# End of the down projection: joins of the first columns as transfers, the last product by tiles of 128 rows, final scaling on three engines

## The reference

```python
def rms_norm(x, gain):
    xf = x.astype(jnp.float32)
    y = xf * lax.rsqrt(jnp.mean(xf * xf, axis=-1, keepdims=True) + NORM_EPS)
    return (y * gain.astype(jnp.float32)).astype(x.dtype)

def squared_relu_mlp(h, w_up, w_down):          # w_down: 8192 x 2048
    u = jax.nn.relu(jnp.einsum('bsd,df->bsf', h, w_up))
    return jnp.einsum('bsf,fd->bsd', u * u, w_down)

    x = x + squared_relu_mlp(h, w_mlp_up[layer], w_mlp_down[layer])
return rms_norm(x, ln_final)
```

## Time and profile before

| | before |
|---|---|
| median of 3 runs | 2839.78 us (2839.66 to 2840.45) |
| the profiled execution's own time | 2841.27 us |
| its span | 2839.8 us |
| granted TensorE clock, mean | 0.997 |
| TensorE busy | 2801.2 us (99%) |
| VectorE busy | 1884.5 us (66%) |
| ScalarE busy | 1181.7 us (42%) |
| GpSimd busy | 345.2 us (12%) |
| last matmul starts | 2823.47 us |
| last of the eight final scalings ends | 2834.99 us |

### The profile page before, as it was taken

The page is one execution under the profiler, slowest core; times in us unless marked ns, Lnnn a source line. Parts: engine busy times, 40 slices in busy tenths (PEclk is TensorE's granted clock), DMA queues, the critical chain, the costliest instruction groups (busy, mean ns, idle before and its releaser), DMA issues.

```text
span 2839.8 us, 42734 instructions
## 1 busy us (share of the span) xinstructions
PE 2801.2 (99%) x16624; PEld 2424.8 (85%) x16624; DVE 1884.5 (66%) x2073; ACT 1181.7 (42%) x1375; POOL 345.2 (12%) x400
## 2 busy tenths in 40 slices
PE   8999999999999999999999999999999999999997
PEld 5888777788889988889888899999998788888886
DVE  7545777755454443434445788888863888888888
ACT  5433433433454332423334365555553333333334
POOL 4000000000001123200111421212113100000001
PEclk9999999999999999999999999999999999999999
DMA  5333222232347874423333699999987756656555
GB/s 164 96 86 93 75 68 79 64 82 78 111 137 212 234 217 122 169 90 110 129 118 110 211 249 258 246 250 246 252 240 256 257 195 221 222 207 221 207 215 132
DMA packets 466144, 477.78 MB, mean 168 GB/s; under 512 B 10832, under 2 KB 369264, under 8 KB 465904
## 3 DMA queue, kind: packets, MB, share of 16 engines
q1 hardware_dynamic: 427136, 346.66, 39.9%
q0 software_dynamic: 38896, 129.56, 15.6%
HBM read 366.60 MB, written 81.79 MB: 158 GB/s over the span
## 4 chain that ended last, share of the span: by engine, by line
PE 91%; DVE 4%; DMA 2%; ACT 2%; issue 1%; POOL 0%; SPq 0%; DVEq 0%; ACTq 0%
PE slab_ps L1004 12%; PE slab_ps L1006 12%; PE slab_ps L1005 12%; PE down_ps L1651 7%; PE down_ps L1653 6%; PE down_ps L1652 6%; PE mix_ps L1594 6%; PE mix_ps L1593 6%; PE mix_ps L1595 6%; PE mix_ps L1006 2%; PE mix_ps L1005 2%; PE mix_ps L1004 2%; PE down_ps L1004 2%; PE down_ps L1006 2%; PE down_ps L1005 2%
## 5 line engine op out<-in xcount | busy, mean ns | idle before, releaser
L1004 PE MATMUL slab_ps<-act_hi,w_hi 128*128 128x512 f32 (+2 forms) x1928 | 721.4, 374 | 15.4 <-DVE act_lo L2421 10.6
L1006 PE MATMUL slab_ps<-act_hi,w_lo 128*128 128x512 f32 (+2 forms) x1928 | 698.5, 362 | 0.0
L1005 PE MATMUL slab_ps<-act_lo,w_hi 128*128 128x512 f32 (+2 forms) x1928 | 698.4, 362 | 0.0
L1679 ACT ACTIVATE w_hi<-w_raw 128x2048 fp32r<-128x2048 f32 x152 | 290.9, 1914 | 550.3 <-PE slab_ps L1006 414.9
L2369 DVE TENSOR_TENSOR w_lo<-w_raw,w_hi 128x2048 fp32r<-128x2048 f32 x152 | 349.4, 2298 | 233.4 <-ACT w_hi L1679 232.7
L1004 PEld LDWEIGHTS slab_ps<-act_hi,w_hi 128*128 128x128 f32 (+1 forms) x1928 | 364.0, 189 | 80.3 <-issue 23.7
L1006 PEld LDWEIGHTS slab_ps<-act_hi,w_lo 128*128 128x128 f32 (+1 forms) x1928 | 363.9, 189 | 57.9 <-issue 1.0
L1005 PEld LDWEIGHTS slab_ps<-act_lo,w_hi 128*128 128x128 f32 (+1 forms) x1928 | 364.4, 189 | 54.7 <-issue 5.3
L1651 PE MATMUL down_ps<-half_hi,u_slot 128*128 128x512 f32 x896 | 350.1, 391 | 2.6 <-DMA u_slot<-u_park 2.6
L1653 PE MATMUL down_ps<-half_lo,u_slot 128*128 128x512 f32 x896 | 349.9, 391 | 0.0
L1652 PE MATMUL down_ps<-half_hi,u_slot 128*128 128x512 f32 x896 | 349.8, 390 | 0.0
(11 more groups left out here) (484 smaller groups left out, 4889.7 us busy)
## 6 DMA issues: line engine op xcount, KB each, us to landing
b<-in_w_mlp_down_dram SPq DMA_DIRECT2D x64, 1024.0 KB, 6.7
w_raw<-in_w_in_dram SPq DMA_DIRECT2D x56, 1024.0 KB, 5.6
u_slot<-u_park SPq DMA_DIRECT2D x112, 512.0 KB, 8.4
w_raw<-in_w_mlp_up_dram SPq DMA_DIRECT2D x84, 512.0 KB, 7.8
w_raw<-in_w_cross_kv_dram SPq DMA_DIRECT2D x32, 1024.0 KB, 6.4
u_park<-u_hi POOLq DMA_DIRECT2D x32, 896.0 KB, 6.4
u_park<-u_lo POOLq DMA_DIRECT2D x32, 896.0 KB, 10.1
ucomb<-w_raw POOLq DMA_DIRECT2D x36, 512.0 KB, 7.9
```

Of the source, the lines that this page charges most:

```text
L1004: mm(ps, wh, xh, start=first, stop=False)
L1005: mm(ps, wh, xl, start=False, stop=False)
L1006: return mm(ps, wl, xh, start=False, stop=last)
L1679: fn(w_hi[:, slot], w_raw[:, slot], ACT.Copy).then_inc(on["slab_hi"], 1)
```

## The change

Three things change, all in the last chunk:

1. All seven joins of n = 0 become transfers, and each is issued from GpSimd's queue as soon as the read that it needs is done. Two joins of n = 1 (B21 += B11, T3 += T2) become transfers too. Four joins leave VectorE's order. ScalarE takes the squares of part 0 between its `half_hi` of halves 21 to 24, and waits for 14 of the transfers ahead of the first.
2. The last product (13) runs with the token tile as its outer loop, so the last chunk is taken out of TensorE's loop and written out; its read is split in two (`last_read(0)`, `last_read(1)`), and the squares, the factor and the scaling of tiles 0 and 1 follow one by one.
3. The two pieces (0, 0) and (1, 0) are multiplied by the gains on GpSimd ahead of time and by the row's factor on ScalarE (`final_scaled`); VectorE keeps six pieces.

```diff
-        FINAL_ORDER = [(2, 0), (3, 0), (2, 1), (3, 1), (0, 0), (1, 0), (0, 1), (1, 1)]
+        FINAL_ORDER = [(2, 0), (3, 0), (2, 1), (3, 1), (0, 1), (1, 1)]
+        SQUARES = 3 * NT
...
             for count, (t, n) in enumerate(FINAL_ORDER):
+                if n and t < 2:
+                    store(t, 0, "fin_squared", SQUARES + 1 + t)
                 store(t, n, "fin_out", count + 1)
...
+            products_read(0, T2)
+            join(0, T2, B11)
+            products_read(0, B22)
+            join(0, B22, T1)
+            pool.wait_ge(on["cols0_joined"], 16 * 4)
+            join(0, B22, T2)
+            products_read(0, B21)
+            join(0, B21, B11)
+            products_read(0, T3)
+            join(0, T3, T2)
+            pool.wait_ge(on["cols0_joined"], 16 * 10)
+            products_read(0, T4)
+            join(0, T4, T3)
+            join(0, T1, T3)
+            pool.wait_ge(on["cols0_joined"], 16 * 14)
+            products_read(1, B11)
+            join(1, B21, B11)
             pool.wait_ge(on["half_sums"], 8 * 2 * NCH - 2)
             pool.dma_start(b12[:].rearrange("p j n -> p (j n)"),
                            ln_final.rearrange("(a d) -> a d", a=1).broadcast_to([P, D])).then_inc(on["vec_in"], 16)
-            pool.wait_ge(on["slab_out"], first_cols)
-            join(0, B22, T1)
-            join(0, B21, B11)
-            pool.wait_ge(on["fin_dve"], 1)
-            join(0, T3, T2)
-            pool.wait_ge(on["cols0_joined"], 16 * 6)
-            join(0, T4, T3)
-            join(0, T1, T3)
+            pool.wait_ge(on["cols0_joined"], 16 * 16)
+            products_read(1, T2)
+            join(1, T3, T2)
+            pool.wait_ge(on["fin_squared"], 4)
+            pool.wait_ge(on["vec_in"], 16 * 2)
+            for t in range(2):
+                nc.gpsimd.tensor_tensor(tile_part(t, 0), tile_part(t, 0), gain_part(0), ALU.mult).then_inc(
+                    on["acc_ready"], 1)
...
+            def last_product(c):
...
+                for t in range(2):
+                    for half in range(2):
+                        h = 2 * i + half
+                        if t == 0:
+                            pe.wait_ge(on["slab_lo"], c * 28 + (SLABS + h + 1))
...
-            with pe.Fori(0, NCH) as c:
+            with pe.Fori(0, NCH - 1) as c:
...
+            for n in range(2):
+                for q in range(PROD - n):
+                    product(NCH - 1, n, q)
+            last_product(NCH - 1)
...
+            def final_scaled(t):
+
+                act.wait_ge(on["fin_rstd"], 2 + t)
+                act.wait_ge(on["acc_ready"], 3 + t)
+                fn(first(t), first(t), ACT.Copy, scale=fcols[:, 4, t:t + 1]).then_inc(on["fin_squared"], 1)
...
             for h in range(4, 26):
                 half_hi(NCH - 1, h)
+                if h == 21:
+                    act.wait_ge(on["cols0_joined"], 16 * 14)
+                if 21 <= h < 21 + NT:
+                    t = (h - 19) % NT
+                    final_square(0, t, first(t))
+            half_hi(NCH - 1, 26)
             act.wait_ge(on["slab_out"], done - PROD + 4)
-            act.wait_ge(on["fin_dve"], 5)
+            act.wait_ge(on["fin_dve"], 3)
             squares_of(1, 1, right)
-            half_hi(NCH - 1, 26)
             half_hi(NCH - 1, 27)
...
+            for t in range(2):
+                act.wait_ge(on["slab_out"], done + t)
+                final_square(2, t, left(t))
+                final_rstd((t,))
+            for t in range(2):
+                final_scaled(t)
...
+            join(1, T4, T3)
+            dve.wait_ge(on["fin_dve"], 5)
+            last_read(0)
             dve.wait_ge(on["vec_in"], 16 * 2)
             for place, (t, n) in enumerate(FINAL_ORDER):
                 if place == 1:
-                    join(1, T4, T3)
-                if place == 2:
-                    read(NCH - 1, 13, last=True)
-                final_tile(t, n, 1 if t >= 2 else 2)
+                    last_read(1)
+                final_tile(t, n, 1 if t >= 2 else 2 + t)
```

More of the change, by code:

```diff
@@ L976, in _ @@
                     main_again(2 * j + 3)
-            first_cols = SLABS + 2 * PROD * NCH - PROD
+            done = SLABS + 2 * PROD * NCH
             def join(n, to, q):
@@ L982, in join, with products_read @@
                     pool.dma_start(acc[n][to][:, t], acc[n][q][:, t], accum_op=ALU.add).then_inc(on["cols0_joined"], 16)
+            def products_read(n, q):
+                pool.wait_ge(on["slab_out"], done - PROD * (2 - n) + q + 1)
+            products_read(0, T2)
[15 more added lines that the diff above has]
+            join(1, B21, B11)
             pool.wait_ge(on["half_sums"], 8 * 2 * NCH - 2)
@@ L1654, in product @@
                     ins.then_inc(on["slab_mul"], 1)
-            with pe.Fori(0, NCH) as c:
+            def last_product(c):
+                i = 2 * PROD - 1
+                bank = down_ps[(1, 0, 2, 3)[i % 4]]
+                pe.wait_ge(on["slab_out"], c * 14 + (SLABS + i - 3))
+                for t in range(2):
[3 more added lines that the diff above has]
+                            pe.wait_ge(on["slab_lo"], c * 28 + (SLABS + h + 1))
+                        wh, wl = half_w[0][h % 4], half_w[1][h % 4]
+                        for j in range(2):
+                            uh, ul = (u_slot[T4][:, part, 2 * half + j, t * P:(t + 1) * P] for part in range(2))
+                            first, last = half == 0 and j == 0, half == 1 and j == 1
+                            mm(bank[:, t], uh, wh[:, j], start=first, stop=False)
+                            mm(bank[:, t], ul, wh[:, j], start=False, stop=False)
+                            ins = mm(bank[:, t], uh, wl[:, j], start=False, stop=last)
+                    ins.then_inc(on["slab_mul"], 1)
+            with pe.Fori(0, NCH - 1) as c:
                 for n in range(2):
@@ L2312, in final_bias, with final_rstd @@
                                   bias=fcols[:, 3, t:t + 1]))
-            def final_rstd(a, done):
+            def final_rstd(tiles):
                 act.wait_ge(on["fin_squared"], squares.n)
-                for t in (a, a + 1):
+                for t in tiles:
                     chain.put(fn(fcols[:, 4, t:t + 1], fcols[:, 2, t:t + 1], ACT.Ln, scale=1.0 / D,
@@ L2320, in final_rstd @@
                 chain.sync()
-                fn(fcols[:, 4, a:a + 2], fcols[:, 4, a:a + 2], ACT.Exp, scale=-0.5).then_inc(on["fin_rstd"], 1)
-                act.wait_ge(on["fin_rstd"], done)
+                both = slice(tiles[0], tiles[-1] + 1)
+                fn(fcols[:, 4, both], fcols[:, 4, both], ACT.Exp, scale=-0.5).then_inc(on["fin_rstd"], 1)
+            def final_scaled(t):
+                act.wait_ge(on["fin_rstd"], 2 + t)
+                act.wait_ge(on["acc_ready"], 3 + t)
+                fn(first(t), first(t), ACT.Copy, scale=fcols[:, 4, t:t + 1]).then_inc(on["fin_squared"], 1)
             def squares_of(part, pair, of):
@@ L2344, in _ @@
             squares_of(2, 1, left)
-            final_rstd(2, 1)
-            act.wait_ge(on["fin_dve"], 8)
+            final_rstd((2, 3))
+            act.wait_ge(on["fin_dve"], 4)
             squares_of(1, 0, right)
-            act.wait_ge(on["cols0_joined"], 16 * 10)
-            squares_of(0, 0, first)
             final_bias(0)
-            act.wait_ge(on["slab_out"], done)
-            squares_of(2, 0, left)
-            final_rstd(0, 2)
+            for t in range(2):
[4 more added lines that the diff above has]
+                final_scaled(t)
         @block.vector
@@ L3299, in read @@
                         dve.wait_ge(on["fin_dve"], JOINED_BEFORE[q_])
+                    elif q_ == B21:
+                        dve.wait_ge(on["cols0_joined"], 16 * 16)
+                    elif q_ == T3:
+                        dve.wait_ge(on["cols0_joined"], 16 * 18)
                 tt(acc[n][q_], acc[n][q_], blocks(bank), ALU.add).then_inc(on["slab_out"], 1)
             def beside_product(c, q, last=False, sums=True):
[L3304 to L3308, removed]
                 if not (last and q == 13):
```

23 lines of the change are left out of this document (9 added, 14 removed).

## The result

The changed kernel takes 2845.39 us (median of 18 runs, 2842.87 to 2849.29) against 2839.99 (18 runs, 2838.47 to 2842.63): a ratio of 1.0019, with a 95% interval of 1.0013 to 1.0025, so it is slower by 5.4 us or about 0.2%. The forecast was 2840.3 with a range up to 2842.5.

A forecast was written before the change was run, and what follows sets the result against it. TensorE was taken to bound nearly all of the kernel, stores the end: second scaling 2827.8 + 10.55 + 2.0 = 2840.35, 0.55 over the earlier span, put on the 2839.78 median: 2840.3, range 2837.7 to 2842.5.

The forecast's parts named there:

- The stores bound the end: Last stretch: stores at 1.51 us a piece are slower than VectorE's scalings; seven after the second scaling take 10.55, closing 2.0.
- The multiplies: GpSimd's two gain multiplies: each holds up VectorE's next two-operand addition 2.3 us if busy, moving the end from 2838.15 to 2840.35.
- The written-out chunk: TensorE's last chunk outside its loop: costed at nothing; as a rival, one stall of 1.2 us either way, 0.5 in 10.
- The tile order: Product 13 by tiles: tile 0 ready at 2820.98, tile 1 at 2823.70 as before; costs nothing by itself.
- scaling on ScalarE and GpSimd: Final scaling: moving two scalings off VectorE earns nothing more, since stores are slower than VectorE.
- The step that failed: Four transfers following the read of product 6 land near 2796.2, hidden by 1.4 us before ScalarE asks at 2797.65.
- if ScalarE stops at half 21: A sign, ScalarE waiting for the transfers at half 21, that would show the prediction wrong; no such wait was expected.
- My sum: Second scaling at 2827.8, plus 10.55 for seven stores and 2.0 for closing: 2840.35, 0.55 us more than the span before.
- Rival 2: Late transfers hold ScalarE at half 21 and starve TensorE if landing after 2803.8; slowest landing 2800.9, 2841.2; 0.5 in 10.
- The prediction's own estimate in that rival: A landing at 2800.9 delays VectorE's low parts by some 0.8 us and gives 2841.2.

The follow-up runs named there:

- v4: The kernel before, with only the last chunk's 14 products written out behind TensorE's loop; ratio to before 1.0002, tail 54.05 us.
- v7: v3 with the last product in the old order, weight halves outside tiles, both half reads waiting for the whole product; tail 54.50 us, ratio to before 1.0001.
- v3: The changed kernel with ScalarE's wait for the 14 transfers and its part-0 squares two weight halves later; tail 52.95 us, ratio to before 1.0000.
- v1: The changed kernel without GpSimd's two multiplies and ScalarE's two scalings, VectorE scaling all eight pieces; tail 54.03 us, ratio to before 1.0003.
- v11: The changed kernel with GpSimd's queue not waiting for B22 += T1 ahead of product 5's transfers, B22 += T2 last; tail 54.96 us, ratio to before 1.0003.
- v5: The changed kernel with GpSimd's two multiplies replaced by two memsets of a free accumulator; tail 55.98 us, ratio to before 1.0006.
- v6: The changed kernel with one of GpSimd's two multiplies, VectorE scaling piece (1, 0) whole; tail 56.78 us, ratio to before 1.0016.
- v10: The changed kernel with GpSimd's two multiplies held back until half 27's low part is made; tail 58.72 us, ratio to before 1.0016.
- v9: v3 without GpSimd multiplies or ScalarE scalings, half 27's high part before part-1 squares, VectorE's scalings spread between last joins; median 2837.47 us, ratio to before 0.9991.

## Why the prediction was wrong

**What held.** The stores bound the end: in every run in which VectorE scales in the order of the change, the end of the second scaling plus 12.55 us gives the span to 0.1 us. The multiplies block VectorE's two-operand additions, 2.2 us each (3.43 and 3.40 against 1.22), near the place where I put them. The written-out chunk costs nothing (v4). The tile order is worth 1.55 us (v7 against v3), and scaling on ScalarE and GpSimd earns nothing that the stores would show: in v1 VectorE does all eight, and its second scaling, 2825.64, plus 12.55 is 2838.2 against a span of 2838.1.

**The step that failed** is "After the change the same four follow the read of product 6 ... so they land near 2796.2 ... They are hidden, by 1.4 us". I took the read of product 6 as the only thing ahead of the four transfers. Ahead of them in the same queue stand two waits for transfers: B22 += T1, then T3 += T2. With the first landing 9.3 us after issue, T3 += T2 is issued at 2782.0 instead of with its read at 2779.3, and its own landing takes until 2791.3. The four are issued at 2791.66, that is 6.9 us later than I took, and land 0.8 us more slowly. On the clock of before they landed at 2803.8 and not 2796.2: 7.6 us later. ScalarE waited 6.19 us for them, and VectorE began the low part of half 22 3.7 us late (20.3 us after the read of product 6 starts, and 16.6 in v3). The prediction had named this sign itself: wrong "if ScalarE stops at half 21". v11 takes the first wait off the queue and sends B22 += T2 last, and the tail falls from 58.4 to 55.0. My sum, 2840.35 on the clock of before, is a tail of 54.7. So the rest of the sum was right and the loss beyond it is the queue's.

**How the delays add up.** From the low part of half 22 to the second scaling VectorE has no gap above 0.15 us in any run whose squares stand at half 21. The time of that stretch and 12.55 us for the stores give the whole tail (times worked out from VectorE's timeline in each run):

| kernel | low part of half 22 starts, us after the read of product 6 starts | from there to the end of the second scaling, us | with 12.55 | tail |
|---|---|---|---|---|
| v1_vector_scales | 20.4 | 21.2 | 54.1 | 54.0 |
| v5_memset | 22.3 | 21.2 | 56.0 | 56.0 |
| v6_one_multiply | 20.9 | 23.4 | 56.9 | 56.8 |
| after | 20.3 | 25.6 | 58.4 | 58.4 |
| v10_multiplies_after | 21.6 | 24.6 | 58.8 | 58.7 |
| v11_queue_order | 16.9 | 25.6 | 55.0 | 55.0 |

The first column is what the transfers do, the second what the multiplies do: nothing 21.2, one 2.2 more, two 4.4 more, or 3.4 behind the last low part. TensorE's waits, from 0 to 3.3 us, and its lower clock appear nowhere in the sum. They come from the same lateness of VectorE, and in these runs nothing waits for TensorE from there to the end.

**Rival 2 had the transfers and the wrong margin.** It said that TensorE would lose time for landings after 2803.8, and that is where they landed; in v5, v6 and v10 they landed later and TensorE waited 0.6 to 2.0 us. But time is lost earlier than that. What bounds the end is when VectorE reads product 12, and there it had only 2.4 us (see v3). The late transfers delay it by 3.8, so that they cost 1.4 even without multiplies (v1). A VectorE in time would give a tail of 52.7 (read of product 12 at 32.86, 7.3 to the end of the second scaling, 12.55); 3.7 for the transfers and 4.4 for the multiplies, less the 2.4, add 5.7, which is the tail of 58.4. The prediction's own estimate in that rival, 0.8 us for a landing at 2800.9, counts VectorE's low parts and carries on to the measured time: 2.9 us more for a landing at 2803.8 give 2844.1, and the tail of 58.35 is 2844.0 on that clock. I had treated the rival as exclusive of the forecast, and its landing came out three us too early, mostly since it has only one of the two waits.

**How the medians fit.** The tail of the profiled run is 4.2 us longer, the median 5.4. The first square started between 18.2 and 20.2 us after the read of product 6 in the profiles with the squares at half 21 (v11 apart), and the one of the changed kernel is at the early end. That later landings make up its other runs is what this suggests; it was not shown for those runs. It would also fit that the changed kernel's runs spread over 6.4 us and those of before over 4.2.

**Left open.** Why B22 += T1 lands 9.3 us after issue, and 11.4 in v5: a weight load and T2 += B11 are under way beside it, but no run separated them. Nor did a run separate the two things that v11 changes, the wait that is gone and the transfers that no longer stand ahead of T3 += T2.

## What to carry to other kernels

Before work is hung on transfers issued from a queue, walk that queue in order: each wait in it holds back all that follows, and a chain of three dependent transfers costs three landings, not one. Delays that look hidden must be added and set against the slack of the engine that the end waits for. Here that was VectorE's 2.4 us ahead of the read of product 12, and not the larger margin of TensorE; a wait of the busiest engine draws the eye, and the chain that ended last says whether it counts. Arithmetic handed to GpSimd from a VectorE that is busy with two-operand additions gives back what it takes (v1, v10), unless it falls where VectorE is idle (v3). What gained time here was ScalarE's squares placed behind the landings and the first scalings placed ahead of VectorE's last joins (v9).

## What the runs showed of the hardware that was not expected

After TensorE had waited 3.3 us its granted clock was 0.59 and 0.56 in the next two stretches of 2 us, most of it at 1.2 GHz, and a matmul step was 0.43 us; after waits of 0.8 (v11), 1.1 (v6) and 2.0 us (v5) it stayed at 1.00. The 1.9 us that this cost TensorE did not lengthen the kernel. An accumulating transfer of 256 KB within SBUF, some 4 us from issue to landing at best, took 9.3 at most in the changed kernel's profile and 10.2 in that of before, and the same group of two differed by 2 us from run to run.
